# Two-layer decoder trunk: four expert weight pieces requested ahead of the last activation tile's store in the same DMA queue

## What is computed

```python
x = x + mixer(rmsnorm(x, norm_mix[l]))              # ends in  @ w_out
h = rmsnorm(x, norm_ffn[l])
group = argmax(h @ w_rg + b_rg)                      # one group of 4
experts = top_k((h @ w_re + b_re)[group], 2)         # two of its 8 experts
x = x + sum(weight * (silu(h @ w_gate[e]) * (h @ w_up[e])) @ w_down[e])
```

## Time and profile before

| | before |
|---|---|
| time, median of 3 runs (lowest to highest) | 1655.12 us (1652.31 to 1655.31) |
| the profiled execution: its own time | 1655.6 us |
| its span in the trace | 1653.9 us |
| TensorE busy | 1560.3 us (94%) |
| VectorE, ScalarE, GpSimd busy | 715.5, 308.2, 46.8 us |
| DMA | 458.03 MB, mean 277 GB/s |

### The profile page before, as it was taken

One profiled execution on the slowest core, in us unless ns is written; L12 is line 12 of the kernel. 1 busy time (PEld: TensorE's weight loads), 2 busy tenths in 40 slices (PEclk: granted clock), 3 DMA queues, 4 the chain that ended last, 5 costly groups with the idle time before them and its releaser, 6 DMA issues. The chain is left out here.

```text
span 1653.9 us, 19530 instructions
## 1 busy us (share of the span) xinstructions
PE 1560.3 (94%) x7428; PEld 730.9 (44%) x7428; DVE 715.5 (43%) x1550; ACT 308.2 (19%) x640; POOL 46.8 (3%) x62
## 2 busy tenths in 40 slices
PE   8999996999999999989999999997799999999995
PEld 4444452444443444445654444554344444444442
DVE  3222344334343333347265389824333333333335
ACT  2000120100000000022244277822000000000002
POOL 0000000000000000000000000000000000000000
PEclk9999997999999999999899899999899999999998
DMA  6271409999999999955210300072899999999993
GB/s 204 77 266 64 169 26 344 420 421 419 421 420 420 421 421 420 421 199 164 77 55 23 153 2 1 1 271 82 345 421 420 420 420 421 421 420 421 420 420 149
DMA packets 111931, 458.03 MB, mean 277 GB/s; under 512 B 29520, under 2 KB 56144, under 8 KB 62672
## 3 DMA queue, kind: packets, MB, share of 16 engines
q1 hardware_dynamic: 106352, 448.23, 67.5%
q0 software_dynamic: 5472, 8.40, 1.4%
HBM read 461.83 MB, written 6.29 MB: 283 GB/s over the span
## 5 line engine op out<-in xcount | busy, mean ns | idle before, releaser
L968 PE MATMUL ps<-raw,e_xT 128*64 128x512 f32 x2112 | 474.4, 600 | 16.8 <-DMA raw<-in_expert_w_up 16.8
L968 PEld LDWEIGHTS ps<-raw,e_xT 128*64 128x64 f32 x2112 | 154.7, 138 | 322.8 <-issue 321.5
L1105 DVE TENSOR_TENSOR e_sg_hid<-e_sg_hid,ps 64x512 f32<-64x512 f32 x66 | 45.0, 681 | 410.3 <-ACT e_sg_hid L1046 410.0
L1091 DVE TENSOR_TENSOR x_res<-x_res,ps 128x512 f32<-128x512 f32 x272 | 173.9, 681 | 4.3 <-PE ps L1006 2.1
L411 PE MATMUL ps<-c_hT,raw 128*128 128x512 f32 x384 | 165.2, 592 | 0.1
L996 PE MATMUL ps<-raw,e_hT 128*64 128x512 f32 x704 | 163.5, 607 | 1.3
L1054 ACT ACTIVATE e_yhi<-ps,e_wtab 128x512 fp32r<-128x512 f32 x66 | 45.3, 687 | 415.3 <-PE ps L996 415.3
L1046 ACT ACTIVATE e_sg_hid<-ps 64x512 f32<-64x512 f32 x66 | 39.2, 594 | 445.0 <-PE ps L968 445.0
L1777 PE MATMUL ps<-a_spare,raw 128*128 128x512 f32 x256 | 115.8, 609 | 3.8 <-DVE a_spare L1538 3.8
L1006 PE MATMUL ps<-e_yhi,e_pick 64*128 64x512 f32 x528 | 112.0, 421 | 6.5 <-DVE x_res L1091 4.8
L1084 DVE SCALAR_TENSOR_TENSOR e_ylo<-ps,e_wtab,e_yhi 128x512 fp32r<-128x512 f32 x66 | 49.6, 751 | 149.3 <-ACT e_yhi L1054 149.3
(11 more groups left out here) (289 smaller groups left out, 1357.7 us busy)
## 6 DMA issues: line engine op xcount, KB each, us to landing
raw<-in_expert_w_gate SPq DMA_DIRECT2D x128, 1024.0 KB, 25.6
raw<-in_expert_w_up SPq DMA_DIRECT2D x128, 1024.0 KB, 26.9
raw<-in_expert_w_down SPq DMA_DIRECT2D x88, 1024.0 KB, 27.0
e_raw<-in_expert_w_down SPq DMA_DIRECT2D x40, 1024.0 KB, 26.5
raw<-in_conv_w_in SPq DMA_DIRECT2D x11, 1024.0 KB, 9.7
raw<-in_w_kv SPq DMA_DIRECT2D x6, 1024.0 KB, 6.3
raw<-in_conv_w_out SPq DMA_DIRECT2D x1, 4096.0 KB, 19.0
raw<-in_attn_w_in SPq DMA_DIRECT2D x4, 1024.0 KB, 5.3
```

The costliest lines, as they stand in the source:

```text
L968: mm = pe.matmul(ps_gu[C - C * i:2 * C - C * i, :], xT[:, q % 2, k, u * C:(u + 1) * C], ring(m, L, p)[:, kk * F:(kk + 1) * F], start=(k == ...
L1091: return dve.tensor_tensor(x, x, bank[:], ALU.add).then_inc(done, 1)
```

## The change

SP asks for pieces 8 to 10 in the loop over the tiles instead of after it: ahead of the wait and the store of the last tile, as soon as `w_out` is free. Piece 11, which was asked for after the first rows had landed, goes with them. After the first rows only pieces 16 and 17 are left. Both layers use the same code.

```diff
--- before.py
+++ after.py
@@ -534,10 +534,11 @@
     def sync_ring(self, sp):
 
         for t in range(NT):
+            if t == NT - 1:
+                sp.wait_ge(self.s_o, 2 * NT + 1)
+                prefetch(sp, self.m, self.L, range(8, 12))
             sp.wait_ge(self.s_xn, t + 1)
             sp.dma_start(self.m.rows_x[self.L][t * P:(t + 1) * P, :], self.xn[:, t % 2, :]).then_inc(self.s_out[t % 2], 16)
-        sp.wait_ge(self.s_o, 2 * NT + 1)
-        prefetch(sp, self.m, self.L, range(8, 11))
 
     def tensor(self, pe, feats, w):
 
@@ -1161,7 +1162,7 @@
                 load(E + j, sp.value_load(m.ovf_e[0:1, j + 1:j + 2], min_val=0, max_val=E - 1))
 
             sp.wait_ge(r.s_rows[0], 16)
-            prefetch(sp, m, L, (11, *range(NR0, NR)))
+            prefetch(sp, m, L, range(NR0, NR))
             if L == 0:
                 with nc.allow_non_contiguous_dma(reason="small vectors"):
                     sp.dma_start(m.kv_scale[:, 0, :], m.a["norm_kv"].rearrange("(k p) -> p k", p=P)).then_inc(m.kv_gain, 16)
```

## The result

| | before | after |
|---|---|---|
| median of 10 runs each (lowest to highest) | 1653.7 us (1650.1 to 1655.31) | 1658.55 us (1655.16 to 1660.47) |
| profiled execution: own time, span | 1655.6, 1653.9 us | 1659.43, 1657.7 us |

The changed kernel takes 1.0031 times as long, with a 95% interval of 1.0022 to 1.0039: about 5 us slower, where 2.4 us faster was forecast. The page hardly shows it: TensorE is busy for 1556 instead of 1560 us, and one idle time stands out.

A forecast was written before the change was run, and what follows sets the result against it. It took the first expert stage as bound by an unbroken DMA weight stream. Layer 0's restart -0.1, its stream -1.95 and layer 1's restart -0.4 made -2.4 us: 1652.7 us, chance 0.50, own range 1650.5 to 1655.5, whole range 1649.2 to 1659.0.

The forecast's parts named there:

- The restarts: TensorE's start on the first gathered rows in each layer: 0.1 us sooner in layer 0, 0.4 us in layer 1.
- The store lands 13.6 us after the first issue: Last store behind four prefetched pieces: 12.35 us for the pieces plus 1.25 for its 512 KB; bounds 12.9 and 15.1.
- GpSimd's reaction: From the store's semaphore to the first gather's issue: taken as 0.6 us, between 0.3 and 0.93.
- The gather, taken as 3.4: First gather on idle engines, read from layer 1's second gather: 3.4 us instead of 7.9 and 8.3; bounds 2.7 and 7.9.
- Two terms of 4.4 and 4.7: At each restart: gather issued some 4.4 us later behind the store, but about 4.7 us shorter on idle engines, nearly cancelling.
- The gain in layer 0's stream: With piece 11 gone from behind the rows, layer 0's first ring piece flows some 2.7 us sooner; 1.95 us stay.
- The last sign of being wrong: In the profile after, layer 0's stream ending no sooner than TensorE's restart moved would show the forecast wrong.
- the second rival: Slower: the gather takes 7.9 us even on idle engines, behind a later store; 4.5 us more per layer, 1661.7; chance 0.16.
- The third: Rival: no effect in layer 0's stream, element loads hold SP anyway; only the two restarts remain, 1654.6; chance 0.14.
- The first rival: Faster: store lands at 12.9 us, GpSimd reacts in 0.3, idle gather needs 2.7; 1649.3 us; chance 0.20.
- The clock: TensorE's granted clock at the first expert's start, 0.50: up to 2.1 us per layer either way; 1 added each side.
- Above 1658.4 is slower: Bound for telling a slower kernel from no change, set by a measurement resolution of 0.2%, 3.3 us.

The follow-up runs named there:

- e9: The change made in layer 0 only, layer 1 left as in the kernel before; ratio 1.0023 against the kernel before.
- e4: The changed kernel with layer 0's two element-wise loads of small vectors issued early, at the router's weights; 1657.24 us, ratio 1.0020 against the kernel before.
- e5: The changed kernel, but in layer 0 SP asks for ring pieces only after the second gather has landed; 1658.12 us, ratio 1.0024 against the kernel before.
- e1: The changed kernel with only pieces 8 to 10 ahead of the last store, piece 11 again behind the first rows; 1651.81 us, ratio 0.9989 against before.
- e3: The changed kernel with only pieces 8 and 9 ahead of the last store, 10, 11, 16 and 17 behind the rows; 1651.09 us, ratio 0.9980 against before.
- e6: The changed kernel with the last tile's store issued by ScalarE in its own hardware queue; 1655.65 us, ratio 1.0009 against the kernel before.

## Why the prediction was wrong

The parts that held: the pieces go out at 242 with nothing kept waiting (241.99). The gather on idle engines takes about half its former time. Layer 0's first ring piece is issued in 0.34 us instead of 3.00, and the gate piece issued at 289.84 lands after 5.2 us, forecast 4.9. That last agreement is luck: the piece was asked for 47.9 us after the projection's end instead of 43.6, behind engines that had just run dry, and not because the stream was ahead. In layer 1 the last move of piece 11 brings nothing.

**The restarts.** The step that put them 0.1 and 0.4 us sooner failed; they came 1.6 and 1.5 us later. "The store lands 13.6 us after the first issue" was 14.5 in both layers. Behind three pieces it is 12.1, so each piece costs 2.4, close to the 2.5 that I had, and the fixed part with the store is 4.9 instead of 3.6. In the stretches that hold the store the engines move only 311 and 315 GB/s, against 418 in a pure stream. That its packets mix there with those of the last pieces is a guess: both are in SP's queue, and the trace does not tell them apart.

```profile
252.00:254.00 2.00, 0.00 (x0) 0.00 (x0) 1.70 (x9) 0.00 (x0) 0.00 (x0) 0.50 1.01 311
254.00:256.00 2.00, 0.00 (x0) 0.00 (x0) 1.75 (x8) 0.00 (x0) 0.00 (x0) 0.50 0.77 315
```

GpSimd's reaction, taken as 0.6, was 0.9. The gather, taken as 3.4, was 3.8 and 4.1. The 3.4 was read from a smaller gather: the second one of layer 1 moved 0.16 MB in its 144 packets, the first one of layer 0 moved 0.27 and that of layer 1 0.25, and in the changed kernel that second gather does land after 3.3 us. The three errors, 0.9, 0.3 and 0.4 to 0.7, all point one way and make the 1.7 us by which layer 0 missed the forecast and the 1.9 of layer 1. I had bounds for each, and the forecast lay on the fast side of the middle in all three. Two terms of 4.4 and 4.7 that cancel leave only their errors; the sign was not known, and 0.50 was too much for that case.

**The gain in layer 0's stream.** "1.95 us reach the end of the stage" failed. The pieces had the margin, but I followed only the pieces. The second gather is issued 2 us after the ring's first piece. Before, it found the engines on tiny packets, and took 6.8 us; after, it stood behind 1 MiB pieces that now flowed at once, took 9.1, and held TensorE before the down product, whose two halves free the next two slots. Before the change, then after it:

```profile
276.44 1.12 PE L952 MATMUL ps<-ident,r_rows 128*128 128x128 f32 x4 [1.50 <-DMA r_rows<-rows_x,r_idx]
277.48 4.76 PE L996 MATMUL ps<-raw,e_hT 128*64 128x512 f32 x16
280.57 2.04 SPq L443 DMA_DIRECT2D raw<-in_expert_w_down  x2
...
281.14 5.24 PE L997 MATMUL ps<-raw,e_hT 128*64 128x512 f32 x16
```

The slots were asked for 42.8 us after the projection's end instead of 38.5. The 4.3 us are 1.6 for the restart, 2.3 for the longer stall and 0.5 for the first half of the down product, which ran wholly at a granted clock of 0.50, less 0.1 for the first products. The engines then ran dry, 33 GB/s from 282 to 284:

```profile
282.00:284.00 2.00, 2.00 (x8) 0.72 (x6) 0.00 (x0) 0.00 (x0) 0.00 (x0) 0.50 0.08 33
```

That this hole is layer 0's loss can be read from the bytes moved in the first 40 us after the projection's end and in the 10 behind them, before and after (columns as in the earlier trace rows):

```profile
242.11:282.11 40.00, 22.20 (x144) 11.09 (x142) 21.60 (x82) 6.96 (x9) 3.14 (x3) 0.70 0.77 283
282.11:292.11 10.00, 8.56 (x44) 3.25 (x42) 2.10 (x4) 1.28 (x2) 0.00 (x0) 1.00 1.00 397
...
241.96:281.96 40.00, 18.25 (x128) 9.90 (x126) 21.60 (x82) 6.96 (x9) 3.14 (x3) 0.69 0.80 292
281.96:291.96 10.00, 10.00 (x44) 3.26 (x42) 0.75 (x1) 0.69 (x1) 0.00 (x0) 0.88 0.64 234
```

After 40 us the changed kernel is 0.4 MB ahead, after 50 it is 1.3 MB behind (e9, with the same code in layer 0, 1.0), about 3 us of the stream, and it stays 1.3 to 1.4 behind for the next 350 us. So the stream's early gain was there, and the hole took more than it. Part A grew by 2.8, and e9 puts layer 0's loss at 3.9 us with an interval of 2.1 to 5.3. Of the 4.3 us by which the slots came later, a margin thus swallowed some 1.1 to 1.5, less than the 1.95 of the forecast, and as a cushion against the delay, not as a gain. The last sign of being wrong that the prediction named, a stream of layer 0 that ends no sooner than the restart moved, came true.

**The rivals.** The sign was the second rival's, but its mechanism was not: it wanted a gather that stays at 7.9 on idle engines, and this was refuted by 3.8 and 4.1. What happened is the forecast's own path with every term of the restart dearer, and one wait more. The third, in which layer 0's stream gains nothing, was the nearest to what layer 0 did, but it had no loss in it. The first rival was refuted by the same landings; no lone gather here took less than 3.2. The estimate of 2.6 us for the gather by the fit of the Trainium skill (DMA: Bandwidth & Descriptors, section on the anatomy of one DMA) does not agree with this trace either, which has 3.8 and 4.1.

**The clock.** It took a small part, within the microsecond that was set aside for it. In layer 0 the first 16 products took 5.66 us, before 5.79, but the down product 5.24 instead of 4.76, with a granted clock of 0.50 from 278 to 284. In layer 1 the first 16 products took 5.23 instead of 4.70, and these 0.5 us and the restart's 1.5 are the 2.0 by which the ring's start there is later.

**The measuring bound.** "Above 1658.4 is slower" stood on the first three runs. Against the ten runs of before the change is 0.31% slower.

**Size and sign.** 1658.55 lies inside the range that was given, at the end that the slower rival had widened; the forecast's own range, 1650.5 to 1655.5, missed it.

What stays open is what the stall alone costs layer 0. The sum above divides the delay of the slots in one trace, but no run removes the stall and leaves the rest: e4's is no smaller than e9's with the same code, and e5 takes it away by holding the ring, so that it has moved 10.2 MB after 40 us instead of 11.7.

## What to carry to other kernels

A small transfer that someone waits for should be looked at together with every byte that is in flight when it is issued, not only with those ahead of it in its queue; here moving bulk ahead of it bought back 4 us on the next small transfer and cost more. The best amount to prefetch was not all or nothing, but what lands just when the consumer's other condition is met: two pieces, by which the store lands about as the indices are ready, though by the times three (e1) are not told apart from two (e3). Before crediting a wait's removal, find the next condition under it (here the block's end, 2.2 us below), and when a stream speeds up, list the other transfers that used its gaps.

## What the runs showed of the hardware

A transfer issued into a saturated stream took 7.7 to 9.3 us to land whichever queue it was in: SP's own (9.3), ScalarE's (8.2 and 8.5) or GpSimd's (7.7 to 9.1, up to 10.2 right behind another gather), while a store with nothing ahead of it needs 2.6 to 3.0 and a lone gather 3.2 to 4.2. In e6 the first 3 us of that passed before its first packet. I had expected a queue of its own to help a store more than the 1.1 us that it did.
